# Columns by load, x scaled in halves, two roundings moved to ScalarE: the first norm of a two-block transformer kernel

## The reference

```
h = concatenate([meta, x])                      # L = 272 tokens
lower_bounds = cumsum(softmax(lb_logits))
u = rms_norm(h, mix_pre_g)
proj = u @ w_in                                 # hq, hf, hi, hg, cq, ckv, kpe, gates
y_a = hgrn2_mixer(hq, hf, hi, hg, lower_bounds, hg_norm_g) @ w_hg_o
y_b = mla_mixer(cq, ckv, kpe, q_a_norm_g, w_q_b, kv_a_norm_g, w_kv_b, cos, sin) @ w_mla_o
h = h + rms_norm((gate_a * y_a + gate_b * y_b) @ w_out, mix_post_g)
h = h + rms_norm((silu(gt) * up) @ w_ffn_out, ffn_post_g)
```

## Time and profile before

| | |
|---|---|
| three runs | 963.73 us median (961.78 to 967.8) |
| profiled execution | 961.15 us, span 959.3 us |
| mean granted clock of TensorE | 0.973 of full speed |
| VectorE, ScalarE, GpSimd busy | 526.2, 470.6, 618.6 us |

### The profile page before, as it was taken

How to read it: one execution, slowest core, us unless ns; L and a number is a source line. 1 busy time by engine, 2 the same in 40 slices (tenths; PEclk the granted TensorE clock), 3 DMA queues, 4 the chain that set the end, 5 groups by cost and what they waited for, 6 DMA issues and landing times.

```text
span 959.3 us, 16864 instructions
## 1 busy us (share of the span) xinstructions
PE 884.5 (92%) x6758; PEld 842.9 (88%) x6758; DVE 526.2 (55%) x1095; ACT 470.6 (49%) x909; POOL 618.6 (64%) x360
## 2 busy tenths in 40 slices
PE   3999899999998998999999997999989889998985
PEld 2987599989997898999999997999888889997885
DVE  5213111189955826755331114988983659799655
ACT  3535555642346434643444444345558454544673
POOL 4521454545556898799998897866852877664051
PEclk9999999999999999899999998999979989998997
DMA  9522543443432355365555672754220527454001
GB/s 259 164 78 88 176 132 91 131 117 104 133 107 73 129 175 177 110 197 177 186 177 159 184 220 58 221 156 150 90 88 1 176 56 219 141 157 147 1 1 44
DMA packets 133991, 125.97 MB, mean 131 GB/s; under 512 B 6405, under 2 KB 131962, under 8 KB 133914
## 3 DMA queue, kind: packets, MB, share of 16 engines
q1 hardware_dynamic: 133360, 124.17, 42.1%
q10 hardware_dynamic: 554, 0.73, 0.2%
HBM read 123.70 MB, written 1.05 MB: 130 GB/s over the span
## 4 chain that ended last, share of the span: by engine, by line
PE 78%; DVE 9%; ACT 5%; POOL 4%; DMA 3%; issue 2%; SPq 0%; ACTq 0%; DVEq 0%
PE PS L577 21%; PE PS L579 20%; PE PS L578 20%; PE PS L813 3%; DMA ring<-in_w_in 3%; POOL w_lo L1068 2%; PE PS L568 2%; ACT w_hi L1190 1%; PE PS L962 1%; PE PS L934 1%; PE PS L991 1%; DVE zoneB L1910 1%; PE PS L779 1%; DVE zoneB L1632 1%; DVE PS L1855 1%
## 5 line engine op out<-in xcount | busy, mean ns | idle before, releaser
L1068 POOL TENSOR_TENSOR w_lo<-ring,w_hi 128x1024 fp32r<-128x1024 f32 (+1 forms) x235 | 540.2, 2313 | 267.1 <-ACT w_hi L1190 255.4
L577 PE MATMUL PS<-x_hi,w_hi 128*128 128x256 f32 (+2 forms) x1560 | 460.4, 295 | 23.9 <-POOL x_lo L1078 9.3
L579 PE MATMUL PS<-x_hi,w_lo 128*128 128x256 f32 (+2 forms) x1560 | 447.6, 287 | 0.0
L578 PE MATMUL PS<-x_lo,w_hi 128*128 128x256 f32 (+2 forms) x1560 | 446.6, 286 | 0.0
L577 PEld LDWEIGHTS PS<-x_hi,w_hi 128*128 128x128 f32 (+1 forms) x1560 | 297.7, 191 | 29.5 <-issue 26.1
L578 PEld LDWEIGHTS PS<-x_lo,w_hi 128*128 128x128 f32 (+1 forms) x1560 | 297.0, 190 | 1.6 <-issue 0.5
L579 PEld LDWEIGHTS PS<-x_hi,w_lo 128*128 128x128 f32 (+1 forms) x1560 | 297.2, 191 | 0.0
L1190 ACT ACTIVATE w_hi<-ring 128x1024 fp32r<-128x1024 f32 (+1 forms) x231 | 233.5, 1013 | 84.8 <-PE PS L579 79.1
L1173 ACT ACTIVATE zoneA<-PS 128x272 f32<-128x272 f32 (+4 forms) x80 | 31.7, 397 | 142.1 <-PE PS L579 141.1
L1855 DVE SCALAR_TENSOR_TENSOR PS<-zoneA,cols,PS 128x256 f32<-128x256 f32 x240 | 98.5, 480 | 0.1
L1173 ACT ACTIVATE zoneB<-PS 128x256 f32<-128x256 f32 (+4 forms) x115 | 40.9, 379 | 86.6 <-DVE PS L1822 39.4
(11 more groups left out here) (275 smaller groups left out, 1218.7 us busy)
## 6 DMA issues: line engine op xcount, KB each, us to landing
ring<-in_w_in SPq DMA_DIRECT2D x58, 1024.0 KB, 5.4
ring<-in_w_ffn_in SPq DMA_DIRECT2D x22, 1024.0 KB, 5.1
ring<-in_w_out SPq DMA_DIRECT2D x12, 1024.0 KB, 5.2
ring<-in_w_ffn_out SPq DMA_DIRECT2D x16, 704.0 KB, 4.7
ring<-in_w_mla_o SPq DMA_DIRECT2D x4, 1024.0 KB, 5.1
ring<-in_w_hg_o SPq DMA_DIRECT2D x4, 1024.0 KB, 5.1
ring<-in_w_kv_b SPq DMA_DIRECT2D x2, 1024.0 KB, 5.5
ring<-in_w_q_b SPq DMA_DIRECT2D x2, 768.0 KB, 4.5
```

The costliest lines, as they stand in the source:

```text
L577: mm(out_, hi_w, hi_x, start=start, stop=False)
L578: mm(out_, hi_w, lo_x, start=False, stop=False)
L579: return mm(out_, lo_w, hi_x, start=False, stop=stop)
L1068: sub(lo_w, src, hi_w, ALU.subtract).then_inc(sem("w_lo"), 1)
```

## The change

1. The fourteen vectors and the tap weights are laid out beforehand, outside the kernel, as the columns of one array (`columns`, 128x373). ScalarE's queue loads the first 125 columns straight into `cols`, third behind x1 and the meta tokens, which have moved there from SP's queue. The 248 tap columns are loaded on SP's queue among the late things. The three transposes of `vec_rows` on TensorE and their copies on ScalarE go. ORDER loses three entries. The meta rows of the second block get a tile of their own, `meta_rows`.
2. ScalarE sums the squares of the meta rows, behind x0's, in the place of VectorE.
3. The scaling of x is done in two halves of 512 columns on both engines, with a semaphore for each half; the transposes of groups 0 to 3 wait for the first, 4 to 7 for the second.
4. BY_DVE = 2: VectorE rounds only the two pieces of c0. The two of c1 are rounded by ScalarE, behind the eight `x_hi`.
5. The exponentials of lb go from behind `x_hi` to behind the last copy of the wkvb linears on ScalarE, and a warm-up of Sqrt goes with them; VectorE's four operations on lb stand just ahead of the attention steps. GpSimd waits for the late loads before its first taps.

```diff
+BY_DVE = 2
-ORDER = [("start", 0)]
-ORDER += [(n, i) for n, k in (("c0", 2), ("c1", 2), ("kpe", 1)) for i in range(k)]
+ORDER = [(n, i) for n, k in (("c0", 2), ("c1", 2), ("kpe", 1)) for i in range(k)]
...
-ORDER += [("start", i) for i in range(1 + DC, 4 + DC)]
+ORDER += [("start", DC + 1)]
...
-            sp.dma_start(m_tok[0:META, 0, :], a["meta_tokens"]).then_inc(sem("m_in"), 16)
             sp.dma_start(const[:, 0:2 * P], a["constants"][:, 0:2 * P]).then_inc(sem("const_in"), 16)
...
-            for l in range(DEPTH2):
-                sp.dma_start(vec_rows[0:TAPS * CC, 1 + l, :],
-                             a["conv_w_2"][l].rearrange("j (c p) -> (j c) p", p=P)).then_inc(sem("late_in"), 16)
+            sp.dma_start(cols[:, N_VEC:N_COLS], a["columns"][:, N_VEC:N_COLS]).then_inc(sem("late_in"), 16)
...
-            pe.wait_ge(sem("vec_in"), 16 * len(VEC_LIST))
-            done(nc.tensor.transpose(PS[:, 0, 0:N_VEC], vec_rows[0:N_VEC, 0, :], ident[0:N_VEC, 0:N_VEC]))
-            pe.wait_ge(sem("x_nrm"), 3)
             for c in range(DC):
+                if c % 4 == 0:
+                    pe.wait_ge(sem(f"x_nrm{c // 4}"), 3)
...
-            pe.wait_ge(sem("late_in"), 64)
-            for l in range(DEPTH2):
-                g = CHUNK["start", DC + 1 + l]
-                bank_free(g)
-                done(nc.tensor.transpose(PS[:, BANK[g], 0:TAPS * CC], vec_rows[0:TAPS * CC, 1 + l, :],
-                                         ident[0:TAPS * CC, 0:TAPS * CC]))
-            g = CHUNK["start", DC + 3]
+            pe.wait_ge(sem("late_in"), 48)
+            g = CHUNK["start", DC + 1]
...
-                if i < PAIRS:
+                if i < BY_DVE:
                     pool.wait_ge(sem("first_w_hi"), i + 1)
                 else:
-                    pool.wait_ge(sem("w_hi"), i - PAIRS + 1)
+                    pool.wait_ge(sem("w_hi"), i - BY_DVE + 1)
...
-            at = 0
-            for name, n in VEC_LIST:
-                v = a[name]
-                v = v.rearrange("a b -> (a b)") if len(v.shape) == 2 else v
-                act.dma_start(vec_rows[at:at + n, 0, :], v.rearrange("(c p) -> c p", p=P)).then_inc(sem("vec_in"), 16)
-                at += n
+            act.dma_start(m_tok[0:META, 0, :], a["meta_tokens"]).then_inc(sem("m_in"), 16)
+            act.dma_start(cols[:, 0:N_VEC], a["columns"][:, 0:N_VEC]).then_inc(sem("cols_in"), 16)
...
+            act.wait_ge(sem("m_in"), 16)
+            af(x_nrm[0:META, 2, :], m_tok[0:META, 0, :], ACT.Square, accum_out=x_sums[0:META, 2:3]).then_inc(sem("x_sums"), 1)
...
-            af(x_nrm[:, 0, :], x_tok[:, 0, :], ACT.Copy, scale=x_rs[:, 0:1]).then_inc(sem("x_nrm"), 1)
-            take("start", 0, cols[:, 0:N_VEC], n=N_VEC)
-            out_of_psum(act, "start", 0)
+            for half in range(2):
+                cols_ = slice(512 * half, 512 * half + 512)
+                af(x_nrm[:, 0, cols_], x_tok[:, 0, cols_], ACT.Copy, scale=x_rs[:, 0:1]).then_inc(sem(f"x_nrm{half}"), 1)
+            act.wait_ge(sem("cols_in"), 16)
...
-            act.wait_ge(sem("lb_shift"), 2)
-            af(lb_e0, lb_e0, ACT.Exp).then_inc(sem("lb_exp"), 1)
-            af(lb_e1, lb_e1, ACT.Exp).then_inc(sem("lb_exp"), 1)
-
-            warm(ACT.Sqrt)
+            for i in range(BY_DVE, PAIRS):
+                round_piece(i)
...
-            for l in range(DEPTH2):
-                take("start", DC + 1 + l, cols[:, TAP_COL[l]:TAP_COL[l] + TAPS * CC], n=TAPS * CC)
-            take("start", DC + 3, vec_rows[:, 0, :], n=P)
+            take("start", DC + 1, meta_rows[:, :], n=P)
...
+            act.wait_ge(sem("lb_shift"), 2)
+            af(lb_e0, lb_e0, ACT.Exp).then_inc(sem("lb_exp"), 1)
+            af(lb_e1, lb_e1, ACT.Exp).then_inc(sem("lb_exp"), 1)
             for c in range(HEADS + 2, HEADS + 4):
                 round_piece(SPLIT[part("hg", c)])
...
-            for t, rows, x in ((2, META, m_tok[0:META, 0, :]), (1, P, x_tok[:, 1, :])):
-                v.tensor_scalar(x_nrm[0:rows, t, :], x, x_rs[0:rows, t:t + 1], None, ALU.mult).then_inc(sem("x_nrm"), 1)
-            for i in range(PAIRS):
+            dve.wait_ge(sem("m_in"), 16)
+            for half in range(2):
+                cols_ = slice(512 * half, 512 * half + 512)
+                for t, rows, x in ((1, P, x_tok[:, 1, cols_]), (2, META, m_tok[0:META, 0, cols_])):
+                    v.tensor_scalar(x_nrm[0:rows, t, cols_], x, x_rs[0:rows, t:t + 1], None, ALU.mult)\
+                        .then_inc(sem(f"x_nrm{half}"), 1)
+            for i in range(BY_DVE):
                 src, hi_w, _ = piece_views(i)
                 w_ready(dve, PIECES[i][0])
                 v.tensor_copy(hi_w, src).then_inc(sem("first_w_hi"), 1)
-            out_of_psum(dve, "start", 0)
+            dve.wait_ge(sem("cols_in"), 16)
...
+def columns_of(inputs):
+
+    rows = [np.asarray(inputs[name]).reshape(-1, P) for name, _ in VEC_LIST]
+    return np.ascontiguousarray(np.concatenate(rows + [np.asarray(inputs["conv_w_2"]).reshape(-1, P)]).T)
```

More of the change, by code:

```diff
@@ L304, in bass_blocks @@
         means = sb("means", [P, len(MEANS), P])
-        vec_rows = sb("vec_rows", [P, 3, P])
+        meta_rows = sb("meta_rows", [P, P])
         cols = sb("cols", [P, N_COLS])
@@ L1086, in first_taps @@
                 w = cols[:, TAP_COL[l]:TAP_COL[l] + CC * TAPS].rearrange("p (o j c) -> p o j c", o=1, c=CC)[:, :, :, c]
+                pool.wait_ge(sem("late_in"), 48)
                 out_of_psum(pool, f"L{l}a{c // 2}", c % 2)
@@ L1105, in _ @@
             lo_items("kpe", "hg4")
-            pool.wait_ge(sem("chunk_done"), CHUNK["start", DC + 3] + 1)
+            pool.wait_ge(sem("chunk_done"), CHUNK["start", DC + 1] + 1)
             nc.gpsimd.memset(att_p[:, 0, META + P:2 * P], 0.0)
@@ L1571, in _ @@
             dve.wait_ge(sem("small"), 1)
-            dve.wait_ge(sem("m_in"), 16)
             dve.wait_ge(sem("x1_in"), 16)
-            for t, rows, x in ((2, META, m_tok[0:META, 0, :]), (1, P, x_tok[:, 1, :])):
-                v.tensor_tensor_reduce(out=x_nrm[0:rows, t, :], in0=x, in1=x, scale=1.0, scalar=0.0, op0=ALU.mult,
-                                       op1=ALU.add, accum_out=x_sums[0:rows, t:t + 1]).then_inc(sem("x_sums"), 1)
+            x = x_tok[:, 1, :]
+            v.tensor_tensor_reduce(out=x_nrm[:, 1, :], in0=x, in1=x, scale=1.0, scalar=0.0, op0=ALU.mult,
+                                   op1=ALU.add, accum_out=x_sums[:, 1:2]).then_inc(sem("x_sums"), 1)
             dve.wait_ge(sem("x_std"), 1)
@@ L1613, in split @@
                 v.tensor_copy(dst, src).then_inc(sem(f"hi_{tag}"), 1)
-            dve.wait_ge(sem("lb_exp"), 2)
-            link(v.tensor_tensor(lb_m, lb_e0, lb_e1, ALU.add))
-            link(v.reciprocal(lb_m, lb_m))
-            link(v.tensor_tensor(lb, lb_e0, lb_m, ALU.mult))
-            link(v.tensor_scalar(oml, lb, -1.0, 1.0, ALU.mult, ALU.add))
             for tag, b, first, name in (("cq", 0, 0, "q_a_norm_g"), ("ckv", 1, 2, "kv_a_norm_g")):
@@ L1641, in rope @@
                 ins.then_inc(sem(f"{tag}_roped"), 1)
-            dve.wait_ge(sem("late_in"), 64)
+            dve.wait_ge(sem("late_in"), 48)
             out_of_psum(dve, "wqb", 11)
@@ L1666, in attention_step @@
                     v.reciprocal(r_buf[0:nq, j % 8, 1:2], r_buf[0:nq, j % 8, 1:2]).then_inc(sem(f"{tag}_inv"), 1)
+            dve.wait_ge(sem("lb_exp"), 2)
+            link(v.tensor_tensor(lb_m, lb_e0, lb_e1, ALU.add))
+            link(v.reciprocal(lb_m, lb_m))
+            link(v.tensor_tensor(lb, lb_e0, lb_m, ALU.mult))
+            link(v.tensor_scalar(oml, lb, -1.0, 1.0, ALU.mult, ALU.add))
             def forget(h):
@@ L1835, in _ @@
             rstd("fpost", 1, nrm[:, 0, 0:SEQ])
-            link(v.tensor_copy(hT[:, :, 0:META], vec_rows[:, 0, :].rearrange("p (c t) -> p c t", c=DC)))
+            link(v.tensor_copy(hT[:, :, 0:META], meta_rows[:, :].rearrange("p (c t) -> p c t", c=DC)))
             add_normed(lambda c: ("ffo", c), "ffn_post_g", "h_ready")
@@ L2062, in _ @@
                 assert steps == PLN_DVE
-_INS = ["x", "meta_tokens", "w_in", "b_gate", "lb_logits", "hg_norm_g", "w_hg_o", "q_a_norm_g", "w_q_b",
-        "kv_a_norm_g", "w_kv_b", "w_mla_o", "w_out", "mix_pre_g", "mix_post_g", "ffn_pre_g", "ffn_post_g",
-        "w_ffn_in", "w_ffn_out", "meta_tokens_2", "w_in_2", "conv_w_2", "conv_b_2", "conv_ln_g_2",
-        "conv_ln_b_2", "w_out_2", "post_ln_g_2", "post_ln_b_2"]
+_INS = ["x", "meta_tokens", "w_in", "w_hg_o", "w_q_b", "w_kv_b", "w_mla_o", "w_out", "w_ffn_in", "w_ffn_out",
+        "meta_tokens_2", "w_in_2", "w_out_2", "post_ln_g_2", "post_ln_b_2"]
+def columns_of(inputs):
+    rows = [np.asarray(inputs[name]).reshape(-1, P) for name, _ in VEC_LIST]
+    return np.ascontiguousarray(np.concatenate(rows + [np.asarray(inputs["conv_w_2"]).reshape(-1, P)]).T)
 def kernel(**inputs):
@@ L2078 @@
     arrays, args = {}, {}
-    for name in _INS + ["constants"]:
```

(4 more changed lines are left out.)

## The result

The changed kernel takes 956.07 us (median of seven runs, 953.48 to 957.45); the kernel before took 962.21 in seven. The ratio is 0.992, with a 95% interval from 0.991 to 0.994: 0.8% faster, 7.6 us by the ratio, 6.1 by the medians. 956.6 was forecast. The profiled execution of the changed kernel is the slowest of its seven, 957.45, and has a span of 955.6, with a mean granted clock of 0.966 where that of before had 0.973.

A forecast was written before the change was run, and what follows sets the result against it. TensorE, busy 884.5 of 959.3 us, was taken to bound the kernel, so only its gaps pay. Gains of 5.1 + 0.7 + 1.3 = 7.1 us gave 954.0, plus 2.6 carried over 956.6 us; range 951.5 to 961.5.

The forecast's parts named there:

- The start of the norm: Kernel start: fewer load issues and halved scaling bring the first transpose from 12.04 to 10.1; gain 1.9, bounds 1.2 and 2.6.
- The columns: Kernel start: the one load of 125 columns lands at 7.7 to 10.7, wanted at about 11.0; taken as hidden.
- The casts: Transposes of x: two casts moved off VectorE remove TensorE's whole 3.2 us stall for the first x_lo; nothing else waits.
- The clock at the first chunk: First chunk: again some 2 us of matmuls at half clock; bounds 0.9 plus 0.9 gained, 2.4 lost.
- Taps: Before the next linear: the meta transposes begin where the two tap transposes did; gain 0.7, bounds 0.6 and 0.8.
- The exponentials: First attention step: the Exp table load falls into ScalarE's idle gap after the kv linears; gain 1.3, at least 1.0.
- The sum: Whole kernel: 5.1 for the front, 0.7 for taps and 1.3 for exponentials make 7.1 us.
- A: Rival at the start: the clock comes up during the transposes; gain 8.9, time 954.8; chance 0.14.
- B: Rival at the start: clock down through the first chunk and beyond, or loads 2 us late; time 959.0; chance 0.12.
- C: Rival at the start: VectorE as late as before, or GpSimd's weights the bound; gain 3.9, time 959.8; chance 0.08.
- D: Rival further on: slower than before by TensorE's clock; at a mean of 0.960 the time is 969.1; chance 0.04.
- the signs of being wrong: TensorE waiting for w_lo or ScalarE for loads before 40 us, columns after 12.5, mean clock over 0.004 from 0.973.

The follow-up runs named there:

- e7: The changed kernel with thirteen loads of 8 rows, which nothing reads, added on ScalarE's queue behind the columns' load; first transpose at 13.04 instead of 9.70 us, 958.56 us.
- e5: The changed kernel with x scaled in one piece again and all transposes waiting for it; first transpose at 10.91 instead of 9.70 us, 958.47 us.
- e3: The kernel before with only the third and fourth weight piece moved to ScalarE, behind the eight x_hi; 958.52 us, ratio 0.996 to the kernel before.
- e2: The changed kernel with BY_DVE = 4, so VectorE again rounds the two pieces of c1 ahead of its first x_lo; 960.26 us, ratio 0.997 to the kernel before.
- e10: The changed kernel unchanged, run and profiled once more beside the kernel before on the same chip; 955.44 us against 963.87, ratio 0.992.
- e6: The changed kernel with the meta rows' sum of squares back on VectorE behind x1's; first transpose at 10.36 instead of 9.70 us, 955.72 us.
- e1: The kernel before with only the exponentials of lb and VectorE's operations on it moved, and the Sqrt warm-up gone; 962.09 us against 963.21, ratio 1.000.
- e4: The changed kernel with 24 unused fp32 matmuls of 128x128 at the head of TensorE's list; 955.24 us, ratio 0.992 to the kernel before.
- e8: The kernel of e4 with 20, 26 and 22 more unused matmuls in TensorE's waits ahead of the ffn and two block 2 layers; 949.77 us, ratio 0.987.

## Why the prediction was right

Forecast 956.6, measured 956.07. The mechanism was right, step by step, as follows; that the numbers agree so closely is in part luck. The forecast took 7.1 us from 963.73, the median of three runs. All seven of before have a median of 962.21, so the forecast started 1.5 too high; by the medians the gain was 6.1, so it took off 1.0 too much. The two misses nearly cancel. In the same way the 7.11 at the first attention step is made of a start and casts that gave 0.6 more than forecast and a first chunk that gave 0.5 less. Its steps:

- **The start of the norm**, 1.9 forecast, 2.34 measured. Right in each part: ScalarE's issues held up the Square (e7), the meta Square of 16 rows costs as much as one of 128 (1.06 for either, and 0.18 for the read), the halves give 0.5 (e5). x0 was ready at 5.77, 0.6 before the forecast's 6.4, and the first halves took 0.1 to 0.2 longer than forecast; this is the difference. 5.77 is also the earliest of the seven profiles with this start: in the repeated one the gain is 2.19.
- **The columns** landed at about 8.9 (issued at 1.66, 7.2 us to landing), between the bounds, and hidden: x_hi 0 waited for its transpose.
- **The casts**, 3.2 forecast, 3.33 measured (5.67 - 2.34), and alone 3.3 (e3). Put back, they cost 4.1 to 4.8 (e2). The roundings on ScalarE lay at 16.83, and TensorE waited for no weight at the start. The reload of c0's slot went out at 16.11, 1.6 earlier than before and not under 1, which held up nothing.
- **The clock at the first chunk**: taken as before, it was 0.5 worse. There were 3.3 us of slow matmuls against 2.2; in e10 1.9, and in e6, with the same transposes ahead, 4.3. It varies between executions, within the bounds of the prediction.
- **Taps**, 0.7 forecast, 0.72 measured (5.88 - 5.16).
- **The exponentials**, 1.3 forecast, 1.31 measured (7.11 - 5.80), alone 1.5 at most (e1). VectorE's new wait held up nothing.
- **The sum**, 7.1 forecast, 7.11 at the first attention step. The later program gave 3.4 us of it back in this profile and 1.9 in the repeated one, with its clock. Over all runs the gain by the ratio is 7.6, with an interval from 6.1 to 9.0, so a lasting loss of a us or so is neither shown nor excluded.
- **Rivals.** A (clock up during the transposes) did not happen in either profile; in e4 transposes didn't even keep a clock that was up. B happened in small in one profile, a first chunk slower by 0.5 of the 2.4. C did not happen. D happened in small: the mean clock of the changed kernel's runs went from 0.966 to 0.973, and with it the time by 4 us.

Of the signs of being wrong, one came: the mean clock of the profiled execution was 0.966, 0.007 from 0.973, where 0.004 was the limit. By the forecast's rule (half a us for each us at half clock) that should have eaten the whole gain. Worked out from the two means, it is an estimated 13 us more at half clock, and they went with a loss of 3.4 us, a quarter us each. The rule priced them as if TensorE had been busy in all of them, and spells can begin in its waits (e8). In the repeated profile, where most of the loss is the one dip near 289, in the midst of work, an estimated 3.5 us more went with a loss of 1.9. The others didn't come: TensorE waited for no w_lo before 40 us, ScalarE there for no load but x0, and the columns were early.

One weakness stays. The forecast took the parts one by one, as if each stood alone. e2 shows that they don't: of the start's 2.3 us only 0.9 reach the first matmul unless the casts move as well. In the prediction this was right by order of the sum, not by argument.

## What to carry to other kernels

Read the start of a kernel as a chain of its own: DMA issues stand in an engine's list like any other work, 0.4 us each here, and thirteen put back in front of the first arithmetic cost 3.3 us at the first transpose. An engine with two duties (here VectorE, rounding a weight that isn't there yet ahead of the x_lo that frees a bank) needs its list in the order in which data land. And an edit that gains 1 us is best checked at fixed marks of the trace, since the time of the whole program scatters by several us with TensorE's clock.

## What the runs showed of the hardware that was not expected

- TensorE's clock fell from 2.4 to 1.2 GHz while the engine did nothing but transpose, with one pause of 0.24 us, from 9.8 to 13.2 us, after 24 matmuls that had brought it up (e4).
- Unused matmuls in TensorE's waits, at four places, took 6.3 us by the medians (956.07 to 949.77), or 5.2 by the ratios of the two kernels to the one before, where the change itself gave 6.1 and 7.6.
- Loads of x issued at the same time after the start landed so that its Square began at 5.77 to 5.99 in six profiles (e2, e4, e6, e8, e10 and the changed kernel's first) and at 6.60 in a seventh (e5). A start bound by one load scatters by 0.8 us.
